# A hybrid decoder step on one core: every second unit takes all four heads of C, and the third chunk of each unit goes into the rows of the first

## What is computed

```
s = q . k_all + bias            (per head, or per map for C)
p = softmax(s)                  (for C: p[map 0] - lambda * p[map 1])
o = p . v_all
```

## Time and profile before

| | us |
|---|---|
| median of 3 runs | 1382.98 (1381.21 to 1383.24) |
| the profiled execution | 1387.83, span 1386.0 |
| TensorE busy | 1300.4 (94% of the span), mean granted clock 0.978 |
| VectorE, ScalarE, GpSimd busy | 496.0, 258.4, 59.6 |
| units of the first layer | from 196 to 386 on the span |
| units of the second layer | from 866 to 1052 |

### The profile page before, as it was taken

How to read it: one execution, slowest core, us unless ns; L and a number is a source line. 1 busy time by engine, 2 the same in 40 slices (tenths; PEclk the granted TensorE clock), 3 DMA queues, 4 the chain that set the end, 5 groups by cost and what they waited for, 6 DMA issues and landing times.

```text
span 1386.0 us, 23151 instructions
## 1 busy us (share of the span) xinstructions
PE 1300.4 (94%) x8038; PEld 809.5 (58%) x8038; DVE 496.0 (36%) x1444; ACT 258.4 (19%) x647; POOL 59.6 (4%) x265
## 2 busy tenths in 40 slices
PE   5988899988999999999999999999899999999998
PEld 2544356644566666666666444665456667767775
DVE  1102458876664111011112056777756411101113
ACT  0111124422213110000003212443220311100001
POOL 1000000000001000000001000000000100000000
PEclk9999899998999999999999999999899999999999
DMA  9989989999943768877863687999994366676663
GB/s 350 226 277 260 274 292 370 329 333 347 300 167 111 277 232 299 314 272 262 331 222 138 205 292 276 332 331 349 349 349 173 129 244 212 221 284 212 212 212 137
DMA packets 189646, 363.83 MB, mean 262 GB/s; under 512 B 22928, under 2 KB 140440, under 8 KB 187866
## 3 DMA queue, kind: packets, MB, share of 16 engines
q1 hardware_dynamic: 155040, 345.62, 72.4%
q10 hardware_dynamic: 34490, 16.74, 5.0%
HBM read 354.20 MB, written 58.40 MB: 298 GB/s over the span
## 4 chain that ended last, share of the span: by engine, by line
PE 76%; DVE 9%; DMA 6%; DVEq 3%; issue 2%; ACT 2%; SPq 2%; ACTq 0%
PE psf L1085 22%; PE psf L1524 19%; DMA ring<-in_tiles 5%; PE psf L1386 4%; PE psf L1436 4%; PE psf L1321 3%; PE psf L1277 3%; PE psf L1507 3%; PE psf L1102 2%; PE psf L1397 2%; PE psf L1132 1%; PE psf L1351 1%; PE psf L1164 1%; DVE ranks L1708 1%; DVEq L1711 1%
## 5 line engine op out<-in xcount | busy, mean ns | idle before, releaser
L1085 PE MATMUL psf<-hT,ring 128*128 128x320 f32 x1184 | 328.8, 437 | 3.5 <-DMA ring<-in_tiles 3.2
L1085 PEld LDWEIGHTS psf<-hT,ring 128*128 128x128 f32 x1184 | 224.0, 191 | 111.2 <-issue 15.9
L1524 PE MATMUL psf<-big,ring 128*128 128x320 f32 x1024 | 278.9, 433 | 4.1 <-DVE big L1981 2.1
L1524 PEld LDWEIGHTS psf<-big,ring 128*128 128x128 f32 x1024 | 193.5, 190 | 90.4 <-issue 5.5
L1981 DVE TENSOR_TENSOR big<-sq 128x320 f32<-128x320 f32 x64 | 31.5, 492 | 248.8 <-ACT sq L1054 248.5
L1622 DVE TENSOR_SCALAR rstd<-psf,adaT 128x256 f32<-128x256 f32 x32 | 15.4, 482 | 250.1 <-PE psf L1524 234.9
L1012 ACT ACTIVATE sq<-xT 128x320 f32<-128x320 f32 x32 | 15.0, 470 | 321.5 <-DVE xT L1626 321.5
L1386 PE MATMUL psf<-oT,ring 128*128 128x320 f32 x256 | 71.6, 435 | 2.2 <-DVE oT L1844 1.0
L1054 ACT ACTIVATE sq<-psf 128x320 f32<-128x320 f32 x64 | 28.0, 437 | 238.9 <-PE psf L1085 224.6
L1277 PE MATMUL psf<-big,qs 128*32 128x512 f32 x512 | 66.7, 616 | 3.7 <-ACT zT L858 2.2
L1321 PE MATMUL psf<-big,ptbuf 128*32 128x128 f32 x2048 | 65.9, 283 | 0.1
(11 more groups left out here) (212 smaller groups left out, 1303.3 us busy)
## 6 DMA issues: line engine op xcount, KB each, us to landing
ring<-in_tiles SPq DMA_DIRECT2D x266, 512.0 KB, 4.7
big<-in_cache_a SPq DMA_DIRECT2D x64, 768.0 KB, 7.2
out_cache_a<-in_cache_a SPq DMA_DIRECT2D x64, 768.0 KB, 6.2
big<-in_pool_bk SPq DMA_DIRECT2D x128, 192.0 KB, 5.3
big<-in_pool_bv SPq DMA_DIRECT2D x128, 192.0 KB, 6.9
big<-in_pool_cv SPq DMA_DIRECT2D x192, 64.0 KB, 5.4
big<-in_pool_ck SPq DMA_DIRECT2D x128, 64.0 KB, 4.5
big<-in_pool_ck ACTq DMA_DIRECT2D x128, 64.0 KB, 5.3
```

The costliest lines, as they stand in the source:

```text
L1085: ins = pe.matmul(ps[:, 0:T], ring[:, s, k, :], rhs[:, k, :], start=k == 0, stop=k == KD - 1)
L1524: ins = pe.matmul(bank[6 + m % 2][:, 0:T], ring[:, s, k, :], uT[:, KD * q + k, :], start=q + k == 0, stop=q == 3 and k == KD - 1)
```

## The change

The chunks are shared out anew. Even units are **light**: three chunks, no C. Odd units are **heavy**: three chunks of A or B and both chunks of C, `chunks = [0, 1, 3, 4, 2]`. A heavy unit of the first half takes all four heads of C of its own sequence (1, 3, 5, 7); in the second half sequences are swapped in pairs (`n % NB ^ 1`), so that the heavy units are those of 0, 2, 4, 6. `QUAD` says which strip of 32 rows a chunk has: chunk 2 shares strip 0 with chunk 0. Its 16 query columns stand in columns 16 to 31 of its weights, with zeros beside them, so that both add up in one PSUM strip; its values are a matmul of its own with the same probabilities as weights, into another bank. The two chunks of C have strips 2 and 3, and a light unit has 64 rows instead of 128. `big` becomes four equal regions for the keys and values of A and B, and one each for C's keys and values, with whole rows of 1024 bytes; only heavy units load them, and SP alone issues them. Two late projections instead of one stand before the first unit, into banks 4 and 3; they wait once for the last sum of the modulation (`ada_set`). The double item moves from unit 11 to unit 10. `osb` and `turn_out` get a second part, for chunk 2. The normalization of C's heads is split by prompt and sample instead of by pair of heads (not shown). The bias rows and the constants are laid out to match (not shown).

```diff
@@ -142,8 +142,12 @@
+QUAD = [0, 1, 0, 2, 3]
@@ -181,14 +185,24 @@
-        self.n, self.b, self.s, self.second = n, n % NB, n % 2, n >= NB
...
+        self.n, self.s, self.second, self.heavy = n, n % 2, n >= NB, n % 2 == 1
+        self.b = n % NB ^ 1 if self.second else n
...
-SLOTS = [*([n] for n in range(11)), [11, 12], [13], [14], [15], [ITEMS]]
+        self.chunks = [0, 1, 3, 4, 2] if self.heavy else [0, 1, 2]
+        self.rows = P if self.heavy else 2 * G
...
+SLOTS = [*([n] for n in range(10)), [10, 11], [12], [13], [14], [15], [ITEMS]]
@@ -224,16 +238,15 @@
-        ck_in, cv_in = ([kv[:, s, at:at + NPG * P].rearrange("p (j w) -> p j w", j=NPG) for s in range(2)]
-                        for at in (CK_AT, CV_AT))
+        k_in, v_in = ([big[:, at + 2 * A_W * s:at + 2 * A_W * s + A_W].rearrange("p (j w) -> p j w", j=NPG) for s in range(2)]
+                      for at in (0, A_W))
+        ck_in, cv_in = (big[:, at:at + C_W].rearrange("p (j w) -> p j w", j=NPG) for at in (4 * A_W, 4 * A_W + C_W))
@@ -453,10 +469,10 @@
-            return bank[5 if i else 3]
+            return bank[(4, 3)[i] if i < 2 else 5]
@@ -527,29 +543,28 @@
-            def load_c(l, u, at, half, which=range(NPG)):
-                load_pages(l, at, a["pool_cv" if half else "pool_ck"], P * u.second, (ck_in, cv_in)[half][u.s],
-                           (ld_ck, ld_cv)[half][u.s], which)
...
+            def load_c(l, at, half):
+                load_pages(l, at, a["pool_cv" if half else "pool_ck"], (ck_in, cv_in)[half], (ld_ck, ld_cv)[half])
@@ -608,9 +623,6 @@
-                    if d in (6, 7):
-                        at = pages(0, CHECKED) if d == 6 else at
-                        load_c(l, UNIT[0], at, d - 6)
@@ -620,7 +632,7 @@
-                        load_c(l, UNIT[1], at, d - 13)
+                        load_c(l, at, d - 13)
@@ -645,15 +657,15 @@
-                        load_c(l, u, at, 0)
...
+                    if u.heavy:
+                        load_c(l, at, 0)
@@ -666,7 +678,8 @@
-                    load_c(l, then, was, 1, range(NPG // 2 if then.second else NPG))
+                    if then.heavy:
+                        load_c(l, was, 1)
@@ -771,18 +784,19 @@
+                        pool.tensor_copy(bass.AP(first.tensor, first.offset, [list(first.ap[0]), [Q_STEP, 3], [1, NT]]),
...
-                    for g in range(4):
+                    for g in range(4 if u.heavy else 0):
@@ -930,30 +945,19 @@
-                def load_c_keys(u, at):
-                    for j in range(NPG):
-                        act.dma_start(ck_in[u.s][:, j, :],
-                                      a["pool_ck"][ds(at[j] + l * N_PHYS, 1), :, P:2 * P].rearrange("o p w -> (o p) w")
-                                      ).then_inc(ld_ck[u.s], 16)
-                def load_c_values(u, at):
-                    for j in range(NPG // 2, NPG):
-                        act.dma_start(cv_in[u.s][:, j, :],
-                                      a["pool_cv"][ds(at[j] + l * N_PHYS, 1), :, P:2 * P].rearrange("o p w -> (o p) w")
...
+                feature(LATE[1], late_bank(1))
@@ -987,19 +991,10 @@
-                        at = pages(UNIT[u.n + 3].b, CHECKED)
-                        load_c_keys(UNIT[u.n + 3], at)
...
-                        act.wait_ge(u_o.sem, u_o.done(l, u.n))
-                        load_c_values(UNIT[u.n + 2], was)
@@ -1262,79 +1259,94 @@
-                        for c in range(4):
+                        if q == 2 and u.n == 1:
+                            pe.wait_ge(z_set.sem, z_set.done(l, MADE_AT[KC + 1]))
+                        for c in u.chunks:
                             if q < 2:
                                 rhs = (k_in[u.s][:, 4 * q:4 * q + 4, P * c:P * c + P] if c < 3
-                                       else ck_in[u.s][:, 4 * q:4 * q + 4, :])
+                                       else ck_in[:, 4 * q:4 * q + 4, P * (c - 3):P * (c - 3) + P])
                             else:
-                                rhs = zT[:, u.k + c if c < 3 else u.kc, t0:t0 + NT]
-                            masked = u.second and c < 3
-                            ins = pe.matmul(psf[G * c:G * c + G, 512 * q:512 * q + w], qs[:, u.s, G * c:G * c + G], rhs,
-                                            start=True, stop=not masked)
-                            if q == 2 and not masked:
-                                ins.then_inc(u_s.sem, 1)
+                                rhs = zT[:, u.k + c if c < 3 else KC + c - 3, t0:t0 + NT]
+                            masked, g = u.second and c < 3, G * QUAD[c]
+                            ins = pe.matmul(psf[g:g + G, 512 * q:512 * q + w], qs[:, u.q_of(c)], rhs,
+                                            start=c != 2, stop=c != 0 and not masked)
+                            if q == 2 and c and not masked:
...
+                    for j in range(NPG // 2, NPG):
+                        at = P * j - 512 if u.heavy else r * j
+                        ins = pe.transpose(bank[4][:, at:at + r], page(j), ident[0:r, 0:r])
+                    pe.transpose(bank[2][0:TS, 256:256 + r], znew[0:r, z0:z0 + TS], ident[0:r, 0:r])
+                    if u.heavy:
+                        pe.wait_ge(u_out.sem, u_out.free(l, u.n))
+                        pe.sem_inc(passed, 1)
                     for j in range(NPG // 2):
-                        ins = pe.transpose(bank[3 + j // 4][:, P * (j % 4):P * (j % 4) + P], S[:, 0, P * j:P * j + P], ident[:])
+                        ins = pe.transpose(bank[3 if u.heavy else 4][:, r * j:r * j + r], page(j), ident[0:r, 0:r])
                     ins.then_inc(u_tp.sem, 1)
...
+                    if u.n == 0:
+                        pe.wait_ge(z_set.sem, z_set.done(l, MADE_AT[LATE[1]]))
+                    elif not u.heavy:
+                        pe.wait_ge(u_out.sem, u_out.free(l, u.n))
                     values_wait(u)
...
-                        for c in range(4):
+                        for c in u.chunks:
+                            g = G * QUAD[c]
                             if j < NPG:
-                                lhs = PT[:, j, G * c:G * c + G]
-                                rhs = v_in[u.s][:, j, P * c:P * c + P] if c < 3 else cv_in[u.s][:, j, :]
+                                lhs = ptbuf[:, u.rows * j + g:u.rows * j + g + G]
+                                rhs = v_in[u.s][:, j, P * c:P * c + P] if c < 3 else cv_in[:, j, P * (c - 3):P * (c - 3) + P]
                             else:
-                                v0 = u.v + P * c if c < 3 else u.vc
-                                lhs, rhs = PT[0:TS, j, G * c:G * c + G], vs[0:TS, v0:v0 + P]
-                            ins = pe.matmul(bank[3][G * c:G * c + G, 0:P], lhs, rhs, start=j == 0, stop=j == NPG)
-                            if j == NPG:
-                                ins.then_inc(u_o.sem, 1)
+                                v0 = u.v + P * c if c < 3 else VC + P * (c - 3)
+                                lhs, rhs = PT[0:TS, j, g:g + G], vs[0:TS, v0:v0 + P]
+                            ins = pe.matmul(bank[4 if c == 2 else 3][g:g + G, 0:P], lhs, rhs, start=j == 0, stop=j == NPG)
+                            if j == NPG and c:
+                                ins.then_inc(u_o.sem, 1 if u.heavy else 2)
...
-                    pe.matmul(bank[3][:, P:P + 64], osb[:], turnO[:], start=True, stop=True).then_inc(u_ot.sem, 1)
+                    r, w = u.rows, 10 * NT if u.heavy else 4 * NT
+                    pe.matmul(bank[3][:, 256:256 + w], osb[0:r, 0:P], turnO[0:r, 0:w], start=True, stop=True)
+                    pe.matmul(bank[3][:, 256 + 4 * NT:256 + 6 * NT], osb[0:r, P:2 * P], ident[0:r, 2 * NT:G],
+                              start=True, stop=True).then_inc(u_ot.sem, 1)
@@ -1443,7 +1455,9 @@
-                chunk(MID[l][0], late_bank(0), hT)
+                pe.wait_ge(ada_set, 1 + max(ada_group(t) for t in PROJ[l] if t[0] in ("mix", "mlp")))
+                for i in range(2):
+                    chunk(MID[l][i], late_bank(i), hT)
@@ -1454,10 +1468,10 @@
-                    if u.n + 1 < len(LATE):
...
                         pe.wait_ge(i_logit.sem, i_logit.done(l, slots[0]))
-                        i = u.n + 1
@@ -1827,12 +1843,15 @@
-                    dve.tensor_scalar(osb[:], bank[3][:, 0:P], rs[:, u.s, 0:1], par_all[:, l, P_COEF:P_COEF + 1],
-                                      ALU.mult, ALU.mult).then_inc(u_oset.sem, 1)
+                    dve.tensor_scalar(osb[r, 0:P], bank[3][r, 0:P], rs[r, u.s, 0:1], par_all[r, l, P_COEF:P_COEF + 1],
+                                      ALU.mult, ALU.mult)
+                    dve.tensor_scalar(osb[0:G, P:2 * P], bank[4][0:G, 0:P], rs[0:G, u.s, 0:1], None, ALU.mult
+                                      ).then_inc(u_oset.sem, 1)
```

(23 more changed lines are left out.)

158 lines of the change are left out of this document (80 added, 78 removed).

## The result

The changed kernel takes **1500.28 us** (median of 4 runs, 1498.72 to 1500.76); beside it the kernel before took 1382.10 (median of 4). The ratio is 1.0861, 95% interval 1.0832 to 1.0890: slower, as forecast, at 13 us above the predicted 1487. The profiled execution took 1500.04 with a span of 1498.3, against 1387.8 and 1386.0 before: +112.2, where the sum said +104.5. (The medians differ by 118.2: the profiled execution before was 5.7 above its median, the one after lies at it.

What follows compares the result with a forecast made beforehand. TensorE's own work was taken to set the units' pace, transfers close behind. Terms from strips (+119.7) to transposes (-4.0) summed to +104.5 us, giving a median of 1487 us; range 1465 to 1511, or 1462 to 1525 with the first two rivals.

Steps and rivals of the forecast that it cites:

- Strips: Logits and values: two chunks in one strip run one after the other, 3.74 us a unit, 119.7 us in 32 units.
- Rival 1: Clock falls more often, perhaps one 3.4 us stretch at half clock in each unit: 1542 us; chance 6%.
- Rival 3: Weight loads not hidden in a shared strip, 2.6 us more a unit in logits and values: 1571 us; chance 2%.
- Turning: Second matmul of `turn_out` for chunk 2's outputs, 0.16 us in each of 32 units: +5.1 us.
- scaling: VectorE scales chunk 2 separately, 0.2 us, showing the 18 times TensorE waits for `osb`: +3.6 us.
- transposes: In light units nine transposes have 64 columns, each 0.03 us shorter: -4 us.
- The waits for `nmxi` (-5.0) and `ptbuf` (-4.0): TensorE's waits before late pieces and for the new tokens' probabilities vanish under longer logits and values: -5.0 and -4.0 us.
- The head of unit 8 (-3.7): Waits of 2.2 and 1.5 us at unit 8 go, as projection and copy come earlier and selection has more time.
- Clock (-8.5): Half-clock stretches after idle time, 17.1 us in all, should vanish with the waits: -8.5 us.
- Transfers and queues, 0: DMA, SP's page issuing and copies for C cost nothing as long as TensorE stays the slowest.
- Rival 2: SP's queue paces the second half, 48 pages a pair of units in 30.2 us: 1498 us; chance 5%.
- rival 4: A strip doesn't limit a round, the 119.7 vanishes; C's longer rows save at most 42 us: 1365; chance 3%.

Runs made afterwards that it cites:

- e1: The kernel before with only chunk 2 moved into chunk 0's strip (one mask less in the second half's units): 1478.3 us, ratio 1.0687.
- e2: The changed kernel with chunk 2 of the light units in the empty strip 2, heavy units unchanged: 1442.3 us, ratio 1.0418.
- e4: The changed kernel without the second scaling on VectorE and the second matmul of `turn_out`, both for chunk 2: 1486.6 us, ratio 1.0738.
- e3: The changed kernel with VectorE's selection right after the ranking, one unit earlier: 1483.9 us, ratio 1.0716.
- e8: The changed kernel without chunk 2's matmuls in logits and values, all else as changed: 1417.5 us, ratio 1.0236.
- e11: The changed kernel without chunk 2's matmuls, its scaling and its turning, and with the selection one step earlier: 1412.8 us, ratio 1.0205.
- e9: The changed kernel with chunk 2 of the light units in its own strip and the selection one step earlier: 1438.5 us, ratio 1.0388.
- e10: The changed kernel without chunk 2's matmuls and with the selection one step earlier: 1414.9 us, ratio 1.0226.
- e5: The kernel before with VectorE's selection right after the ranking, one unit earlier: 1388.9 us, ratio 1.0043 against the kernel before.
- e12: The changed kernel without chunk 2's matmuls, with the selection earlier and B's page rows loaded 1024 bytes wide instead of 1536: 1414.5 us, ratio 1.0219.

## Why the prediction was right, step by step

*Direction and cause: right, and shown.* The shared strip alone gives +95.5 in the kernel before (e1); freeing it for half the units gives 58.0 back (e2).

*Strips, 119.7.* Logits and values now take 3.55 and 3.96 us, 1.76 and 1.92 more: 3.69 a unit, 118.0 in 32. e1 has 117.3 at full clock. The step that carried it, that a strip takes a column in 0.84 ns alone or beside three others, held: strip 0's rounds alone, from 239.91, are 0.43 us apart too. Rival 1 had no part: from 190 to 312 us, with all those rounds, the granted clock never falls. Rival 3 had none: loads of 109 ns go on under rounds of 109 ns in one and the same strip. The rule of the Trainium skill, page "TensorE: Matmul & The Clock Gate", Part 3, that only a load for other row groups overlaps running matmuls, doesn't hold in these rows. The same Part names a second case, a load into a background weight buffer, and the rows don't tell whether this is it.

*Turning 5.1, scaling 3.6, transposes -4.0.* e4 measures 5.8 and 3.8 for the first two. The changed kernel has 1.9 of work more than e1, and 5.8 of that is the turning, so the other differences, the narrow transposes first, come to -3.9. All three were sized well. The two waits more for `osb`, 1.3, were too much: these waits are 13.0 us in all, 2.9 above the kernel before, where the two terms have 4.9. What was left out is the clock: the same two operations cost 5.3 us more by it.

*The waits for `nmxi` (-5.0) and `ptbuf` (-4.0): right,* but for 0.3 both are gone. The double item's stayed, as said, at 2.6.

***The head of unit 8 (-3.7): wrong.*** This step failed. I wrote that the last late projection "and its copy come a unit earlier and the selection has more time". The selection doesn't start earlier; VectorE's program puts it behind unit 6's outputs. What moved away was TensorE's work beside it. The wait became 4.7 in each layer, so +5.7 in place of -3.7, 9.4 off.

***Clock (-8.5): wrong.*** Three stretches at half clock were to vanish. The two behind the waits for `ptbuf`, 318.45 and 984.05 in the earlier trace rows, did. The one at unit 8 didn't, as its wait didn't: before, it held 3.4 us of work in the first layer; now there is one in each layer, 312.08 to 318.91 and 1032.29 to 1039.12, with 6.8 us together, 1.7 more lost where the sum had 1.7 less. And three are new, those behind the waits for `osb` (e4): 4.9 lost, which the sum had at nothing. The double item's gave back 1.6. So the clock gave back 1.8 in all. e3 takes the wait at unit 8 away and gets 8.6 of idle time and 6.7 of clock, which brings the two terms about to where the sum had them. Had I read the order of instructions for what TensorE has to do while the selection runs, and not for what VectorE has, the wait and its clock would have been +7 instead of -5.

The two errors make 16 us (9.4 and 6.7). By the table, work is 1.6 less than the sum's, idle time 6.5 more (9.4 at unit 8, less 2.0 at `osb` and 0.9 elsewhere) and clock 6.7 more, which takes 104.5 to the 116.1 of the units. Outside of them the span was 3.9 shorter. The median is 13 off, and not the 8 by which the sum missed the profiled executions, since I took 4.8 us off for a slow profiled execution, and the one after wasn't slow. The range held 1500, but its upper end doesn't come out of the bounds named: the high bounds with no fall gone add up to 18, 1505 and not 1511.

*Transfers and queues, 0: right for this kernel.* The DMA share fell to 0.77, and nothing waited for C. Rival 2 had SP at 30.2 us for a pair's 48 pages; it took 27.8 (335.93 to 363.76), against 28.3 of TensorE for the units of that time and 27.0 for units 12 and 13. That was close, and e8 and e11 show loads awaited once units are shorter.

*Longer rows of C* brought next to nothing. The queues' time:

```profile
q1 hardware_dynamic: 145840, 358.46, 69.5%
q10 hardware_dynamic: 6890, 4.14, 1.5%
```

71.0% of 1498.3 is 1064 us of the 16 engines; the earlier trace rows give 77.4% of 1386.0, 1073. Some 9 us of the queues' time, not the 42 of rival 4's upper bound.

## What to carry to other kernels

Where narrow matmuls share the array by column strips, count passes per strip: the fullest strip sets the step, and an empty strip elsewhere gives nothing back. Before moving a piece of TensorE's work, look up which wait it covers where it stands now; here the wait that it uncovered was 4.7 us a layer, and taking it away gave 8.2 a layer. A wait's removal is worth what stands next in the same engine's program leaves of it: in four kernels the same edit gave 16 us (e3), 4 us (e9), nothing clear of noise (e10) and a loss of 6 (e5).

## What the runs showed beyond that

- Idle time can cost more than itself. e4's two small operations took 9.6 us of work and waits and another 5.3 by the clock. How long the clock stays down doesn't follow from the wait alone: behind the same 4.7 us at unit 8, TensorE worked 3.2 us at half clock in the changed kernel and 9.1 in e8, without a pause in either. No run shows what sets it.
- The parts of one change don't add up: strips alone +95.5 (e1), all the rest alone +34.6 (e8), together +117.3 to +118.2. The 12 us between are waits that the longer units cover, and the clock behind them: by the table, the rises of the two runs together hold 7.9 more of idle time and 8.5 more of clock than that of the changed kernel.
- A narrower row (1024 for 1536 bytes) left the time the same, within what six runs can tell: 1414.5 against 1414.9 (e12, e10).
